# Moving the first compression round into the input projection of a one-layer decoder step

## The reference

```python
p = rmsnorm(x, norm1_g) @ w_in          # 1024 -> 1816 columns: q, kv_cmp, kv_slc, kv_win, gates, u
kv_slc, kv_win = norm_keys(kv_slc), norm_keys(kv_win)     # RMS norm of each key head
# compression: every block of 64 cached rows becomes one key and one value row
blk = pad_to_blocks(kv_cmp) + cmp_pos_emb
kc = einsum('bnlkd,lde->bnke', blk[:, :, :, 0], w_cmp_k)   # sum over l (64 rows) and d (64 lanes)
vc = einsum('bnlkd,lde->bnke', blk[:, :, :, 1], w_cmp_v)
kc = rmsnorm(kc, k_norm_cmp_g)
# three attention branches (compressed blocks, top-16 selected blocks, window of 512), sigmoid gates
P  = pool_mix(u)                        # multi-scale causal pooling
h  = x + concat(A, P) @ w_out
y  = h + hier_moe(rmsnorm(h, norm2_g))  # 16 experts, 2 of them for each row
```

## Time and profile before

| | us |
|---|---|
| median of 3 runs | 788.08 (780.66, 788.08, 789.23) |
| the profiled execution | 788.33 |
| its span (first to last instruction) | 786.7 |
| PE busy | 730.6 (93%) |
| DVE, ACT, POOL busy | 267.7, 172.1, 186.0 |
| PE's share of the chain of waits | 77% |

### The profile page before, as it was taken

The page is one execution under the profiler, slowest core; times in us unless marked ns, Lnnn a source line. Parts: engine busy times, 40 slices in busy tenths (PEclk is TensorE's granted clock), DMA queues, the critical chain, the costliest instruction groups (busy, mean ns, idle before and its releaser), DMA issues.

```text
span 786.7 us, 16071 instructions
## 1 busy us (share of the span) xinstructions
PE 730.6 (93%) x6460; PEld 411.3 (52%) x6460; DVE 267.7 (34%) x695; ACT 172.1 (22%) x367; POOL 186.0 (24%) x313
## 2 busy tenths in 40 slices
PE   6999998899889787888879999999999999999998
PEld 3555546656566554566735545345555544455542
DVE  1200071355647557766402337311111000111147
ACT  3100031344656533423201101101110011011000
POOL 2000044467667562644100000100000000000050
PEclk9999999989999659999989999999999999999999
DMA  9856645301910892656896019488999999999964
GB/s 282 228 163 210 202 105 116 121 2 56 318 58 17 260 338 65 174 155 186 231 408 271 27 55 357 166 319 318 402 407 419 428 414 424 420 420 419 393 251 144
DMA packets 74479, 191.76 MB, mean 244 GB/s; under 512 B 13718, under 2 KB 48806, under 8 KB 69917
## 3 DMA queue, kind: packets, MB, share of 16 engines
q1 hardware_dynamic: 62565, 154.82, 54.7%
q0 software_dynamic: 9600, 27.77, 10.4%
q10 hardware_dynamic: 2240, 8.13, 2.6%
HBM read 174.09 MB, written 16.70 MB: 243 GB/s over the span
## 4 chain that ended last, share of the span: by engine, by line
PE 77%; DVE 9%; issue 5%; DMA 5%; POOL 1%; ACT 1%; POOLq 1%; SPq 1%; DVEq 0%; ACTq 0%
PE bank L1319 30%; PE bank L879 13%; PE bank L1220 7%; PE bank L923 4%; PE bank L1027 2%; PE bank L876 2%; DMA arena<-in_w_out 2%; PE bank L1303 2%; DVE arena L1946 1%; PE bank L1166 1%; PE bank L1071 1%; PE bank L1040 1%; PE bank L1411 1%; PE bank L1211 1%; PE bank L1240 1%
## 5 line engine op out<-in xcount | busy, mean ns | idle before, releaser
L1319 PE MATMUL bank<-arena,proj 128*32 128x256 f32 (+1 forms) x2352 | 238.7, 483 | 1.3 <-DVE proj L2164 0.8
L1319 PEld LDWEIGHTS bank<-arena,proj 128*32 128x32 f32 x2352 | 103.6, 110 | 96.1 <-issue 77.7
L879 PE MATMUL bank<-arena,amT 128*128 128x454 f32 x256 | 101.1, 553 | 0.8 <-DVE amT L1661 0.8
L2352 POOL DMA_INDIRECT proj<-normed_rows,idx x12 | 11.4, 954 | 309.1 <-PE bank L1303 192.4
L2174 DVE TENSOR_TENSOR proj<-proj,bank 128x256 f32<-128x256 f32 x24 | 10.0, 422 | 209.8 <-PE bank L1319 209.8
L879 PEld LDWEIGHTS bank<-arena,amT 128*128 128x128 f32 x256 | 48.6, 193 | 49.2 <-issue 48.0
L1220 PE MATMUL bank<-arena,amT 128*128 128x512 f32 x128 | 57.8, 608 | 6.6 <-DMA arena<-in_w_out 6.6
L2291 POOL DMA_DIRECT2D arena<-in_cache_slc_kv x96 | 51.5, 536 | 52.5 <-issue 46.0
L1319 PE MATMUL bank<-amT,proj 128*32 128x512 f32 (+1 forms) x336 | 56.5, 532 | 0.0
L1319 PE MATMUL bank<-queries_and_bias,proj 128*32 128x512 f32 (+1 forms) x384 | 56.5, 486 | 0.0
L1220 PEld LDWEIGHTS bank<-arena,amT 128*128 128x128 f32 x128 | 24.5, 196 | 35.5 <-issue 28.7
(11 more groups left out here) (374 smaller groups left out, 1135.7 us busy)
## 6 DMA issues: line engine op xcount, KB each, us to landing
arena<-in_w_up SPq DMA_DIRECT2D x13, 2048.0 KB, 16.7
arena<-in_w_down SPq DMA_DIRECT2D x13, 2048.0 KB, 16.3
arena<-in_w_gate SPq DMA_DIRECT2D x10, 2048.0 KB, 17.1
arena<-in_cache_cmp_kv SPq DMA_DIRECT2D x96, 128.0 KB, 2.2
amT<-in_w_gate SPq DMA_DIRECT2D x3, 2048.0 KB, 14.5
queries_and_bias<-in_w_gate SPq DMA_DIRECT2D x3, 2048.0 KB, 11.7
expert_rows<-proj ACTq DMA_DIRECT2D x11, 512.0 KB, 9.7
arena<-in_w_in SPq DMA_DIRECT2D x3, 1816.0 KB, 7.5
```

The lines of the kernel that those rows point to most:

```text
L879: last = pe.matmul(ps(("in", c, i))[0:n, 0:WC], xnT[:, k, i * P:i * P + n], w_in[c % 2][:, k, :], start=k == 0, stop=k == KC - 1)
L1319: ins = pe.matmul(dst[part, :], rows[:, part], own if q < TRIO else shared, start=start, stop=stop)
```

## The change

- Round 0 of the compression moves into quarters 2 and 3 of the projection: eight steps in the middle of each of the eight products from `(c=2, i=0)` to `(c=3, i=2)`. Its `w_cmp` comes in four quarters of 16 lanes, two buffers in `xh` (`load_quarter`); then both matrices are loaded whole for round 1, after the stores of the pool rows. PSUM banks 4 and 5 are kept for it, the projection rotates over six.
- Pages of sequences 2 and 3 are issued by POOL early, those of 4 to 7 behind round 0's last copy. The position rows are loaded first.
- Round 1 lies in units 1 to 8, and POOL alone makes its copies. `AT_...` move to units 10 to 16 and on. Round 0's read-out (`raw(0)`) moves ahead of the key copies of DVE.
- The head squares go tile by tile through two small buffers, and DVE norms the keys with four operations over all tiles in place of POOL's twenty.
- `w_out` is split: rows 512 to 1023 are loaded in the sample stage to two other places, so that only eight DMAs (2 MB) wait for the end of that stage. Slot 1 of the experts comes free early, so five matrices are loaded before the output projection ends.
- The gain of norm 2 is waited for with `x`; some semaphores are merged; the square of `h` is written elsewhere.

```diff
-CMP_UNITS = [(0, 6), (15, 5)]
+CMP_UNITS = [(0, 0), (1, 8)]
-BEFORE = 3
+EARLY_GROUPS = 8
+QUARTER = 16
+IN_BANKS = (0, 1, 2, 3, 6, 7)
-    idle = [(0, i, s) for i, s in enumerate((2, 3, 4, 5, 0, 1, 6, 7))]
+    idle = [(0, i, s) for i, s in enumerate((2, 3, 4, 5, 1, 0, 6, 7))]
+def compress_within(c, i):
+    k = (c - 2) * TILES + i
+    return share([(0, d) for d in range(HD)], EARLY_GROUPS, k) if k < EARLY_GROUPS else []
-    21, 22, 25, 26, 28, 29, 23, 29
+    10, 11, 13, 14, 15, 16, 12, 16
...
+            def load_quarter(q):
+                for kv, w in enumerate((a["w_cmp_k"], a["w_cmp_v"])):
+                    for par in range(2):
+                        sp.dma_start(w_quarter[q % 2][64 * par:64 * par + 64, kv, :, :], w[:, q * QUARTER:(q + 1) * QUARTER, :])\
+                            .then_inc(ld_quarter[q % 2], 16)
...
-            load_cache(0, 0, 2)
+            for par in range(2):
+                sp.dma_start(posr[64 * par:64 * par + 64, :], a["cmp_pos_emb"]).then_inc(ld_pos, 16)
+            load_cache(0, 2)
+            sp.wait_ge(act_sq, TILES)
+            filled(sp, ("xT", TILES - 1, 1))
+            load_quarter(0)
             filled(sp, ("in", 0, TILES - 1))
             load_win(2)
-            load_cache(0, 2, 2)
+            load_quarter(1)
             filled(sp, ("in", 1, TILES - 1))
             load_win(3)
...
+            for q in (2, 3):
+                sp.wait_ge(chunk_used, QUARTER * (q - 1))
+                load_quarter(q)
+            sp.wait_ge(regrouped, regrouped_at(0, HD - 1))
+            load_later(4)
+            load_later(5)
...
             for b in range(DB):
                 store(out["new_pool_sample"][b, 7:15, :], proj[8 * b:8 * b + 8, 4, CU:CU + 512], st_pool)
+            for par in range(2):
+                filled(sp, ("cmp", 0, par))
+            load_wcmp(1)
+            load_wcmp(0)
...
+                if t == 2:
+                    for k in range(KVH):
+                        filled(sp, ("p_T", NP - 1, k))
+                    filled(sp, ("p_o", NW - 1))
+                    sp.wait_ge(st_out, 16 * N_OUT)
+                    sp.dma_start(w_out_late, a["w_out"][512:768, :].rearrange("(k p) c -> p k c", p=P)).then_inc(ld_wout, 16)
+                    for k in range(2):
+                        src = a["w_out"][768 + P * k:768 + P * (k + 1), :].rearrange("p (h c) -> p h c", h=2)
+                        sp.dma_start(w_out_rows[:, 2 * k:2 * k + 2, :], src).then_inc(ld_wout, 16)
...
-                if n == 4:
+                if n == 5:
                     filled(sp, ("h", TILES - 1, 1))
...
                     for k in range(KC):
+                        if c >= 2 and k == KC // 2:
+                            for r, d in compress_within(c, i):
+                                compress(r, d)
...
+                if r == 0 and d % QUARTER == 0:
+                    pe.wait_ge(ld_quarter[d // QUARTER % 2], 64 * (d // QUARTER // 2 + 1))
+                pe.wait_ge(regrouped, regrouped_at(r, d))
...
-            pe.wait_ge(ld_wout, 16 * 9)
+            pe.wait_ge(ld_wout, 16 * 11)
...
+                    for j, col in enumerate((CSLC, CWIN)):
+                        kk = proj[:, :, col:col + P].rearrange("p t (h d) -> p t h d", d=HD)
+                        inverse = spread(nrm[:, :, 8 + 2 * j:10 + 2 * j].rearrange("p t (h a) -> p t h a", a=1), 3, HD)
+                        link(ve.tensor_tensor(kk, kk, inverse, ALU.mult))
+                        gain = spread(spread(gains[:, 1 + j, :].rearrange("p (a b d) -> p a b d", a=1, b=1), 1, TILES), 2, KVH)
+                        last = ve.tensor_tensor(kk, kk, gain, ALU.mult)
+                    last.then_inc(k_ready, 1)
...
+            raw(0)
...
+            filled(po, ("in", 0, 0))
+            cmp_pages(2)
+            cmp_pages(3)
+            po.wait_ge(ld_pos, 32)
...
+            po.wait_ge(ld_cache, 32 * 16)
+            po.wait_ge(ld_last, 32 * 16)
+            filled(po, ("xT", TILES - 1, 1))
+            po.wait_ge(act_sq, TILES)
             for d in range(HD):
                 regroup(0, d)
             po.wait_ge(regrouped, regrouped_at(0, HD - 1))
             cmp_pages(6)
             cmp_pages(7)
...
-            for d in range(0, HD, 2):
+            for d in range(HD):
                 regroup(1, d)
```

More of the change, by code:

```diff
@@ L414, in hybrid_step @@
         second = sb("second_branch", [P, G, P])
+        qn = [shares[:, :, :].rearrange("p a b -> p (a b)"), second[:, :, :].rearrange("p a b -> p (a b)")]
         pT = [proj[:, 0:4, c:c + 512] for c in (0, CU)]
@@ L856, in xT, with compress @@
                     written(last, ("xT", i, half))
+            def compress(r, d):
+                if d == 0:
+                    for par in range(2):
+                        opened(pe, ("cmp", r, par))
+                    if r == 1:
+                        pe.wait_ge(ld_wcmp, 64)
+                if r == 0 and d % QUARTER == 0:
+                    pe.wait_ge(ld_quarter[d // QUARTER % 2], 64 * (d // QUARTER // 2 + 1))
+                pe.wait_ge(regrouped, regrouped_at(r, d))
+                n = 2 * slots_of(r)
+                for par in range(2):
+                    rows = slice(64 * par, 64 * par + 64)
+                    for kv in range(2):
+                        w = w_quarter[d // QUARTER % 2][rows, kv, d % QUARTER, :] if r == 0 else w_cmp[kv][rows, d, :]
+                        last = pe.matmul(ps(("cmp", r, par))[64 * kv:64 * kv + 64, 0:n], w,
+                                         chunks[r][d % RING][rows, kv, 0:n], start=d == 0, stop=d == HD - 1)
+                    if d == HD - 1:
+                        written(last, ("cmp", r, par))
+                if d < HD - 1:
+                    last.then_inc(chunk_used, 1)
             xT(0)
@@ L942, in _ @@
                 written(last, ("kT", i))
-                for r, d in compress_before(i):
-                    compress(r, d)
             pe.wait_ge(g_ready, 1)
@@ L1211, in projected_sample @@
                         last = pe.matmul(ps(("h", 4, half))[NS * half:NS * half + NS, :], amT[:, k, SEQ:NT],
-                                         w_out[:, k, half * 512:(half + 1) * 512], start=k == 0, stop=k == KC - 1)
+                                         out_matrix(k, half), start=k == 0, stop=k == KC - 1)
                         if k == KC - 1:
@@ L1887, in _ @@
                     weights_of(fourth_at(u, 2))
[L1888 to L1895 removed]
+                if u == sum(CMP_UNITS[1]):
+                    raw(1)
+                    for par in range(2):
+                        taken(ve, ("cmp", 1, par))
+                    ve.tensor_tensor(ktmp, kcr, kcr, ALU.mult).then_inc(kc_sq, 1)
                 beside(u)
```

188 lines of the change are left out of this document (65 added, 123 removed).

## The result

The changed kernel takes **793.55 us** (median of seven runs, 791.28 to 797.07) against 788.08 us for the kernel before (seven runs too, 780.66 to 789.31): ratio 1.009, 95% interval 1.005 to 1.013. It is slower, by about 0.9%. The forecast was 784.5 us, faster by 0.5%. The range held the time, the sign was wrong, and it was not the slower rival (E) that came true. The profiled execution of the changed kernel took 791.28 us (span 789.5), the fastest of the seven.

The account below looks back on a forecast made before the run. PE was taken to set the pace from 7 us to the end. Items 1 to 9 summed to +3.8 us, with item 11 -3.8, from 788.33 to 784.5 us; own range 779 to 792, wider range 774 to 798.

Parts of the forecast that it names:

- rival (E): Units 16 to 23: clock falls after key work stops PE in unit 11 and stays low; 799.5 us, chance 0.12.
- item 2: Projection: w_in's third quarter, behind position and w_cmp loads on SP, lands near 71, wanted at 70.6; +0.7 us (0 to 2).
- item 6: Unit 1: PE stops 8.2 us for w_cmp loaded behind pool stores, plus 1.7 cold restart; +9.9 us (0 to 14).
- Item 1: Projection: eight bursts of eight compression steps added, POOL's copies covered; +15.5 us.
- Rival D: Projection: POOL copies and VectorE two-input operations lock ports in turn, three bursts come 3.5 late; 795 us, chance 0.05.
- Item 3: Transposes before the gate rows: compression steps leave, five tiles then run at 0.8 each; -4.1 us.
- Rival B: Unit 1: w_cmp is there in time, so no added wait; 774.6 us, chance 0.15.
- Item 7: PE's wait before unit 15 goes because round 1's pages load beside projection and mixer; -3.8 us.
- Items 5, 8 and 9: Units 6 to 8 gain steps, +6.0; units 15 to 19 lose them, -15.8; side work moves to 9 to 19, -2.5.
- rival C: Side work hides in fuller units and the clock holds to the end; 776 us, 8.5 below the forecast, chance 0.13.
- Item 10: Key norm moves from POOL to VectorE, four operations, 4.4 us, covered by slack; 0.
- Item 11: Before the output projection: half the output matrix loads in the sample stage, ending PE's wait and cold restart; -7.6 us.

Follow-up runs that it names:

- the quarters behind: Changed kernel with w_in's third quarter issued directly ahead of both w_cmp quarters instead of between them; ratio 0.9988 to the kernel before.
- w_cmp_v early: Changed kernel with w_in's third quarter loaded early and w_cmp_v loaded at the end of round 0, ahead of late pages; ratio 0.9898 to the kernel before.
- units 3 to 10: Changed kernel with w_in's third quarter loaded early, round 1 in units 3 to 10 and side work two units later; ratio 0.9860 to the kernel before.
- side work late: Changed kernel with w_in's third quarter early, round 1 in units 3 to 10, side work back in units 20 to 29; ratio 0.9913 to the kernel before.
- v early, units 3 to 10: Changed kernel with w_in's third quarter early, w_cmp_v loaded at the end of round 0, round 1 in units 3 to 10; ratio 0.9785 to the kernel before.
- stores wait: Changed kernel with w_in's third quarter early and key, value and pooling-state stores held until both w_cmp matrices landed; ratio 0.9954 to the kernel before.

## Why the prediction was wrong, point by point

**The step that failed is item 2.** It put the third quarter of w_in at "near 71, wanted at 70.6", and gave it 0.7 us (0 to 2). It stopped PE 6.17 us, and the half clock behind the stop cost another 2.5: 8.7 us. "A stop before the third quarter of more than 2 us" was among the signs named as wrong, and removing it moves the ratio from 1.009 to 0.997 (0.994 to 1.000), where the forecast was 0.9955. That the rest of the sum comes so near is in part luck, since errors in it cancel, as the list shows. The step failed in three ways. First, the issue came at 65.17, where the item's terms give 62.2 (58.61 plus six issues of 0.6): the old page loads started 2.6 us later (36.58 against 33.97), 1.4 more than the two position loads that the item counts, and took 1.4 us more. Why they did is not shown. Second, the flight took 11.35 us where the item allows 8.8. It counted the bytes ahead (1 MB) but not the megabyte that SP issues 0.6 us behind (nor the fourth quarter of w_in, issued 5.3 us behind): with 2 MB right behind it and none ahead the flight was 9.8 us, in the kernel before 7.5. And third, it priced no cold restart here, although item 6 did so for the very same kind of stop. The windows of the kernel before show 344 GB/s while w_in was in flight there, those of the changed kernel 233 and 307:

```profile
60.00:64.00 4.00, 4.00 (x12) 2.07 (x11) 0.69 (x1) 0.00 (x0) 0.00 (x0) 1.00 0.98 344
```

```profile
64.00:68.00 4.00, 4.00 (x19) 1.99 (x19) 0.00 (x0) 0.64 (x1) 3.41 (x6) 1.00 0.92 233
68.00:72.00 4.00, 2.40 (x26) 1.51 (x22) 0.90 (x2) 0.00 (x0) 1.26 (x3) 1.00 0.98 307
```

The engines were full (0.92 and 0.98) at a lower rate, as they were while w_cmp, in loads of 64 partitions too, was in flight. The Trainium skill (SBUF — State Buffer, Door 1: The DMA port swizzle) says that a tile on 64 partitions reaches half of the ports, some 218 GB/s; this trace agrees (217 to 229 GB/s over 174 to 190 us, with the engines 97% busy and more). The Trainium skill (DMA: Bandwidth & Descriptors, Issuing engines are not separate DMA queues) also says that DMAs started by different engines run on the same 16 DMA engines and interleave; the 2.3 us of "the quarters behind" fit that for transfers of one queue.

- **Item 1**, bursts: 15.5 forecast; 8 x 1.93 = 15.4. Each also breaks the stream of projection records, 16 of which take 6.30 instead of 6.17 us: +1.0 in all, not foreseen. POOL fed every burst in time. Rival D is out.
- **Item 3**, transposes: 3.6 us from the first to the gate rows against 7.9, -4.3 for -4.1. Right.
- **Items 2 and 6 together** set when the load of w_cmp can begin: it is issued at 171.75, the forecast had 162.6. These 9.1 us are item 2 (8.0 over its 0.7) and the 1.0 of item 1.
- **Item 6**, the added wait: right in place and mechanism, mis-sized. From first issue to PE's first step 24.1 us, forecast 22.0; in the runs 22.3 to 24.1. The wait itself read 12.45 and not 8.2 because unit 0 ran at full clock and PE came some 2 us sooner, which gained nothing. The cold restart: 43.1 us from the first to the last step of round 1, 40.8 where no stop led into it ("w_cmp_v early"): 2.3 for 1.7. Rival B (w_cmp in time) is out.
- **Item 7**: no stop for pages is left. Right (in the trace before, the stop itself was 3.05 us and ended at 223.14; the other 0.75 of the 3.8 belongs to item 8, and the sum of the two stays); although it was near: the last cached page released POOL at 179.35, and the first chunk was there at 181.1, 2.3 us before PE wanted it.
- **Items 5, 8 and 9**: the round's place about 10 for 9.8, right; the side work 7.9 for 2.5 by the profiles of its own experiment (4 by its ratios), with round 1 in units 3 to 10. In the changed kernel less of it arrived: from the end of round 1 to the sample stage 73.7 us, forecast 75.5, for the small products still ran partly at half clock (5.76 us for the 32, 4.27 in "units 3 to 10"; the granted clock was 0.74 over 260 to 280). So of rival C's 8.5 us beyond the forecast the changed kernel had 1.8, and E was not true.
- **Item 10**, key norm: no wait of PE, 0 as forecast. POOL's copies beside VectorE's norms became slower, see the last section.
- **Item 11**: 7.6 forecast, 7.2 measured alone. Right. The sample stage took another 1.8 us less than forecast (91.8 for 93.6); 1.4 of it are its first 16 transposes, which ran at full clock this time (1.91 us for 3.28). That was luck, no term foresaw it.

The sum of the misses: +9.1 before the w_cmp load, +2.15 in the load, -0.3 in round 1, -1.8 up to the sample stage, -1.8 in it, -0.6 behind it: 6.75 of the 6.8 us between forecast and profile. The last three, 4.2 us, hid part of the miss. What stays open is the clock of unit 0: "units 3 to 10" and "side work late" are the same program up to unit 10, and one ran its unit 0 at full clock (12 score records in 5.5 us), the other at half (8.41). Where a load ends the next stop this costs nothing; in "v early, units 3 to 10" nothing covers it. The runs don't show what decides it.

## What to carry to other kernels

When a change puts new loads on a queue, price every transfer that PE waits for soon after by its own row: who is ahead of it, what is issued within its flight behind it, and whether that runs at the slow rate; and give each stop of several microseconds its cold restart. A large load that comes late can be moved, but each small load, store or table behind it in the same queue then needs its own deadline checked; starting the consumer two units later was simpler and gained as much. Test a change with several parts by its loads first: here one order of two page loops and a load turned +0.9% into -0.3%, and with w_cmp_v earlier and the round two units later into -2.2%, with the arithmetic untouched.

## What the runs showed of the hardware

- **VectorE and POOL slow each other to 1.5 and 1.8 times.** While VectorE ran its norms of two SBUF inputs, POOL's copies went from 0.58 to 1.05 us each and VectorE's operations from 0.69 to 1.0 to 1.1 us. First POOL with VectorE idle and busy, then VectorE before and beside POOL's copies:

```profile
92.78 1.75 POOL L2311 COPY QB<-arena 128x260 f32<-128x260 f32 x3
...
132.36 3.16 POOL L2311 COPY QB<-arena 128x260 f32<-128x260 f32 x3
```

```profile
129.16 0.68 DVE L1732 TENSOR_TENSOR shares<-proj,nrm 128x512 f32<-128x512 f32 x1
...
131.97 0.99 DVE L1734 TENSOR_TENSOR proj<-second_branch,gains 128x512 f32<-128x512 f32 x1
132.89 1.11 DVE L1732 TENSOR_TENSOR shares<-proj,nrm 128x512 f32<-128x512 f32 x1
```

  From 129.88 to 134.94 VectorE finished five operations (3.4 us alone) and POOL about 4.8 copies (2.8 alone): 6.2 us of work in 5.1 us. So the two are nearer to taking turns than the prediction's rows suggested, though not all the way to the lock of rival D; eight copies took 8.4 us, and the last chunk was there 0.7 us before the last burst came to it.
- **Behind a large unfinished load, issuing itself can take long.** One small store behind the w_cmp load took 12.33 us to issue; in "stores wait", where it was issued after the load had landed, the same store took 0.55. Sixteen page loads behind w_cmp took 16.14. Nobody waited for the store; behind the page loads stood the small load for which PE waited 13 us.

```profile
177.70 12.33 SPq L732 DMA_DIRECT2D out_new_slc_kv_sample<-proj  x1
```

- **After a stop of 1.44 us the clock held, after 6.17 us it was at half** for the first eight records (granted clock 0.50 over 76 to 80), then full again. After stops of 2.22 and 2.38 us in unit 0 ("w_cmp_v early" and "v early, units 3 to 10") the next products ran at half clock too (2.68 us for four, 1.73 at full), but unit 0 did the same in four kernels with only 0.94 us before them, so those two don't show what the stop did.
